# Expert rows added into the residual in place: gathered rows of x, an alternating expert order, and no buffer of expert outputs

## What is computed

```python
# hier_moe: one of 4 groups per token, then 2 of the 8 experts inside that group
g_sel = argmax(h @ w_group)
top_p, top_e = top_k(softmax(exp_logits[g_sel]), 2)      # weights = p_group * top_p / sum
eid = g_sel * 8 + top_e
# expert e on its rows, in blocks of 128:
y = (silu(h @ w_gate[e]) * (h @ w_up[e])) @ w_down[e]
x = x + sum over the token's two experts of weight * y
```

## Time and profile before

| | us |
|---|---|
| median of 3 runs | 3014.01 (3011.21 to 3019.95) |
| the profiled execution, its own time | 3014.33 |
| its span, first to last instruction | 3012.6 |
| PE busy (share of the span) | 2619.9 (87%) |
| DVE, ACT, POOL busy | 1820.9 (60%), 1647.7 (55%), 590.5 (20%) |
| the two experts stages, by their first and last POOL instructions | 1022.5 to 1570.3 and 2387.4 to 2908.9 |
| `lru`, first DVE instruction to last oT store issued | 1577.4 to 2125.9 |
| `finish`, first load issued to the end | 2915.2 to 3012.6 |

### The profile page before, as it was taken

How to read it: one execution, slowest core, us unless ns; L and a number is a source line. 1 busy time by engine, 2 the same in 40 slices (tenths; PEclk the granted TensorE clock), 3 DMA queues, 4 the chain that set the end, 5 groups by cost and what they waited for, 6 DMA issues and landing times. The chain is left out here.

```text
span 3012.6 us, 41660 instructions
## 1 busy us (share of the span) xinstructions
PE 2619.9 (87%) x12246; PEld 2100.4 (70%) x12246; DVE 1820.9 (60%) x3169; ACT 1647.7 (55%) x2260; POOL 590.5 (20%) x795
## 2 busy tenths in 40 slices
PE   6999999999799599999976999999599589999850
PEld 4878878788688477777755777777488467777640
DVE  4555555554456566565636888877465577556546
ACT  5565565554344366565635666675444376555532
POOL 0000000000011344555430000000011255545420
PEclk9999999999899799999987999999799799999985
DMA  3223223331445589789866545451444599877867
GB/s 122 90 91 101 89 91 105 104 107 57 142 155 167 173 295 312 273 281 323 271 218 215 175 166 168 144 171 63 128 154 147 178 350 337 289 264 265 307 237 293
DMA packets 388258, 573.61 MB, mean 190 GB/s; under 512 B 33408, under 2 KB 304000, under 8 KB 384000
## 3 DMA queue, kind: packets, MB, share of 16 engines
q1 hardware_dynamic: 353104, 457.23, 45.8%
q0 software_dynamic: 32688, 105.99, 9.4%
q10 hardware_dynamic: 2304, 8.39, 0.7%
HBM read 449.32 MB, written 122.22 MB: 190 GB/s over the span
## 5 line engine op out<-in xcount | busy, mean ns | idle before, releaser
L1445 DVE TENSOR_TENSOR experts_gu_lo<-carry_raw,experts_gu_hi 128x1024 fp32r<-128x1024 f32 x256 | 296.6, 1220 | 64.4 <-ACT experts_gu_hi L1404 62.4
L1327 POOL DMA_INDIRECT experts_rows<-h_rows,experts_source_now x194 | 269.8, 1391 | 274.0 <-PE experts_ps L1497 129.3
L118 PE MATMUL experts_ps<-experts_gu_hi,experts_hT_hi 128*128 128x512 f32 x760 | 316.3, 416 | 3.0 <-issue 3.0
L119 PE MATMUL experts_ps<-experts_gu_lo,experts_hT_hi 128*128 128x512 f32 x760 | 300.3, 395 | 0.0
L120 PE MATMUL experts_ps<-experts_gu_hi,experts_hT_lo 128*128 128x512 f32 x760 | 299.9, 395 | 0.0
L1404 ACT ACTIVATE experts_gu_hi<-carry_raw 128x1024 fp32r<-128x1024 f32 x256 | 250.2, 1057 | 52.5 <-DMA carry_raw<-in_moe_w_up 42.8
L1456 DVE TENSOR_TENSOR experts_hT_lo<-experts_ps,experts_hT_hi 128x512 fp32r<-128x512 f32 x194 | 133.2, 687 | 240.6 <-ACT experts_hT_hi L1383 233.6
L963 POOL MEMSET route_empty<- 128x512 int32 x2 | 1.1, 564 | 1322.1 <-POOLq L160 1322.1
L118 PE MATMUL route_ps<-route_w_hi,route_src_hi 128*128 128x512 f32 x512 | 208.6, 407 | 45.7 <-DVE route_src_lo L1029 45.7
L1396 ACT ACTIVATE experts_y<-experts_ps,experts_by_block 128x1024 f32<-128x1024 f32 x99 | 110.6, 1117 | 213.8 <-DMA y_rows<-experts_y,experts_target_now 208.4
L119 PE MATMUL route_ps<-route_w_lo,route_src_hi 128*128 128x512 f32 x512 | 203.4, 397 | 0.0
(11 more groups left out here) (322 smaller groups left out, 6757.1 us busy)
## 6 DMA issues: line engine op xcount, KB each, us to landing
carry_raw<-in_moe_w_gate SPq DMA_DIRECT2D x64, 1024.0 KB
carry_raw<-in_moe_w_up SPq DMA_DIRECT2D x64, 1024.0 KB
ahead_wd_raw<-in_moe_w_down SPq DMA_DIRECT2D x64, 1024.0 KB
gla_w_raw<-in_gla_w_in SPq DMA_DIRECT2D x32, 1024.0 KB, 7.3
ahead_wd_raw<-in_lru_w_in SPq DMA_DIRECT2D x32, 1024.0 KB
gla_w_raw<-in_gla_w_in SPq DMA_DIRECT2D x32, 512.0 KB, 5.1
route_src<-oT_rows SPq DMA_DIRECT2D x32, 512.0 KB
x_rows<-route_x_new SPq DMA_DIRECT2D x32, 512.0 KB, 2.9
```

Source lines behind the costliest of these rows:

```text
L118: nc.tensor.matmul(out, w_hi, x_hi, start=first, stop=False)
L119: nc.tensor.matmul(out, w_hi, x_lo, start=False, stop=False)
L1327: pool.indirect_dma_start(rows[:, b], None, h_halves[b], bass.IndirectOffsetOnAxis(source_now[b][:].bitcast(U32), 0))\
L1445: nc.vector.tensor_tensor(gu_lo[:, slot(e), of_part(c)], gu_raw[:, slot(e), of_part(c)], gu_hi[:, slot(e), of_part(c)].bitcast(F32), ALU.s ...
```

## The change

- Experts are taken in the order `ORDER`: expert 0 of each of the four groups, then expert 1 of each, and so on. Lists and weights are looked up by that order.
- Before a block's output is taken, POOL gathers the rows of x that it belongs to into a new buffer `acc`. DVE computes y = output x weight + acc (one instruction, L1396's work moved from ACT and joined with the addition), and POOL scatters y back over the same rows of x.
- `y_rows` is gone. `lru` and `finish` load x and go straight to the norm: no y loads, no additions, and in `lru` no store of x. The early loads of x (and in `finish` of the gain) are gone too, since x is only final when the experts are done. `finish` has 8 buffers for x, and ACT squares tile t+1 before it issues the output of tile t.
- The gathers and the scatter have a bounds check with the limit T - 1: padding places name rows from T upward and are left out of the transfer. Lists are halved in place, and the separate array of sources is gone.

```diff
+ORDER = [g * EPG + j for j in range(EPG) for g in range(GROUPS)]
 def experts
-                n = (words[e // PACK] // PACK_BASE ** (e % PACK)) % PACK_BASE
+                at = ORDER[e]
+                n = (words[at // PACK] // PACK_BASE ** (at % PACK)) % PACK_BASE
...
+            pool.memset(acc[:], 0.0)
+            pool.memset(rows[:], 0.0)
...
                 pool.indirect_dma_start(rows[:, b], None, h_halves[b],
-                                        bass.IndirectOffsetOnAxis(source_now[b][:].bitcast(U32), 0))\
+                                        bass.IndirectOffsetOnAxis(source_now[b][:].bitcast(U32), 0),
+                                        bounds_check=T - 1, oob_is_err=False)\
...
-                pool.indirect_dma_start(y_rows, bass.IndirectOffsetOnAxis(target_now[:].bitcast(U32), 0),
-                                        y[:], None).then_inc(y_stored, DMA)
+                pool.indirect_dma_start(x_rows, bass.IndirectOffsetOnAxis(target_now[:].bitcast(U32), 0),
+                                        y[:], None, bounds_check=T - 1, oob_is_err=False).then_inc(y_stored, DMA)
+            def name_acc(i):
+                if not (isinstance(i, int) and i == -1):
+                    pool.wait_ge(acc_in, nth_acc(i - 1))
+                pool.wait_ge(listed, nth(i - 2))
+                stand(pool)
+                pool.tensor_copy(acc_now[:].unsqueeze(1), by_block[:, bass.ds(i + (LAG - 2), 1), 0:1])\
+                    .then_inc(acc_set, 1)
+            def gather_acc(i):
+                pool.wait_ge(acc_set, nth(i + 1))
+                pool.wait_ge(y_done, nth(i - 1))
+                stand(pool)
+                pool.indirect_dma_start(acc[:], None, x_rows,
+                                        bass.IndirectOffsetOnAxis(acc_now[:].bitcast(U32), 0),
+                                        bounds_check=T - 1, oob_is_err=False).then_inc(acc_in, DMA)
             def each(e, b, g, n):
                 name_rows(0, column, g + 1)
                 gather(0, g + 1)
                 name_targets(g - 1)
+                name_acc(g)
                 store_y(g - 1)
+                gather_acc(g)
                 name_rows(1, column, g + 1)
                 gather(1, g + 1)
                 keep_list(column, g + 1)
...
+            def take_y(i):                      # on DVE, removed from ACT
+                dve.wait_ge(y_ps_done, nth(i))
+                dve.wait_ge(acc_in, nth_acc(i))
+                dve.wait_ge(y_stored, nth_stored(i - 1))
+                dve.wait_ge(listed, nth(i - 2))
+                stand(dve)
+                nc.vector.scalar_tensor_tensor(
+                    out=y[:].rearrange("p (b c) -> p b c", b=2), in0=ps[:, Y:Y + 2],
+                    scalar=by_block[:, bass.ds(i + (LAG - 2), 1), 1].bitcast(F32),
+                    in1=acc[:].rearrange("p (b c) -> p b c", b=2), op0=ALU.mult, op1=ALU.add).then_inc(y_done, 1)
...
             def each(e, b, g, n):               # DVE
                 take_aT(g)
+                take_y(g)
                 take_rows(g + 1, 0)
 def lru
+            def load_x(t):
+                after(sp, h_done, t - 2)
+                sp.dma_start(x[:, t % 2], x_dram[t * P:(t + 1) * P, :]).then_inc(x_in[t % 2], DMA)
-            def combine(t):
-                step(nc.vector.tensor_tensor(x[:, j], x[:, j], y_ab[:, j, 0], ALU.add))
-                nc.vector.tensor_tensor(x[:, j], x[:, j], y_ab[:, j, 1], ALU.add).then_inc(x_done, 1)
 def finish
+            for t in range(NT):
+                after(sp, h_done, t - XD)
+                sp.dma_start(x[:, t % XD], x_dram[t * P:(t + 1) * P, :]).then_inc(x_in[t % XD], DMA)
+                if t == 0:
+                    sp.dma_start(gain[:], norm_w.partition_broadcast(P)).then_inc(gain_in, DMA)
...
+                if t + 1 < NT:
+                    mean_square(t + 1)
                 after(act, h_done, t)
                 act.dma_start(out[t * P:(t + 1) * P, :], h[:, j]).then_inc(stored[j], DMA)
...
-                step(nc.vector.tensor_tensor(x[:, t % XD], x[:, t % XD], y_ab[:, j, 0], ALU.add))
-                nc.vector.tensor_tensor(x[:, t % XD], x[:, t % XD], y_ab[:, j, 1], ALU.add).then_inc(x_done, 1)
```

More of the change, by code:

```diff
@@ L1205, in project_and_route, with experts @@
         m.end()
-def experts(nc, k, stage, h_halves, lists_dram, w_gate, w_up, w_down, y_rows, ahead, after_all):
+def experts(nc, k, stage, h_halves, lists_dram, w_gate, w_up, w_down, x_rows, ahead, after_all):
     with ExitStack() as ctx:
@@ L1436, in _ @@
             take_aT(blocks)
-            for i in (blocks, blocks + 1):
-                take_y(i)
         @block.vector
@@ L1489, in _ @@
             take_aT(blocks)
+            for i in (blocks, blocks + 1):
+                take_y(i)
         @block.tensor
@@ L1769, in _ @@
             after_dma(sp, y_stored, STEPS - 1)
-            for j in range(2):
-                after_dma(sp, x_stored[j], NT // 2 - 1)
         @block.scalar
@@ L2149, in build @@
                               moe_w_down[1])
-            early = FinishEarly(nc, held)
-            experts(nc, k, "experts1", h_halves, lists, moe_w_gate[1], moe_w_up[1], moe_w_down[1], y_rows, ahead,
-                    lambda sp, _: early.load(sp, x2, final_norm))
-            finish(nc, k, x2, y_rows, early, out[0])
+            experts(nc, k, "experts1", h_halves, lists, moe_w_gate[1], moe_w_up[1], moe_w_down[1], x2, ahead,
+                    lambda sp, _: None)
+        finish(nc, k, x2, final_norm, out[0])
 INPUTS = ["x", "gla_norm", "gla_w_in", "gla_w_alpha", "gla_b_alpha", "gla_head_norm", "gla_w_out",
```

139 lines of the change are left out of this document (42 added, 97 removed).

## The result

The changed kernel takes 3070.9 us (median of 4 runs, 3067.8 to 3073.8) against 3015.8 us of the kernel before (4 runs in the same comparison): ratio 1.0183, 95% interval 1.0162 to 1.0204. It is slower by 55 us, where 11 us faster was forecast, and it lies above the range. The profiled run has a span of 3072.1 us.

A forecast was written before the change was run, and what follows sets the result against it. Experts were taken as PE-bound (91 to 93% busy) with late h rows and the output loop behind, one-block runs as weight-bound, finish as nearly DMA-bound. Terms -47 - 4 + 4 - 10 + 15 + 31 = -11 gave 3003 us, range 2950 to 3065.

The forecast's parts named there:

- 1. finish: Final stage: half the bytes per tile and two fewer DVE additions, -47 us, bounds -40 and -50.
- 2. lru: In lru: a shorter start without y loads and additions, steady steps unchanged, -4 us, bounds 0 and -29.
- 3. Ends: Ends of the experts stages: last outputs form a serial chain with the added gather, 2 us a stage, +4 us.
- 4. order: Experts of layer 1: alternating groups mixes one-block and two-block experts, relieving weight loading, -10 us, bounds 0 and -25.
- 5. y on VectorE: Experts: the output moved to DVE makes one-block experts late, half of them charged, +15 us, bounds 0 and +30.
- 6. POOL and the output loop: Experts: POOL's added copy and gather delay second blocks, 1.0 us for each of 31, +31 us, bounds 0 and +124.
- POOL becomes the bound: Experts: two-block experts pay 1.3 us a block, the others 0.9, giving 3068 us; chance 0.2.
- POOL's waits for PE vanish: Experts: sign that POOL limits the kernel, its 67.6 us of waits for PE, between scatter and second gather, disappearing.
- The experts cost nothing: Experts: left-out padding, evened DMA and POOL's room absorb the added work, giving 2957 us; chance 0.25.
- The padding still moves: Experts: out-of-bounds places cost as much as others, 1.5 us per one-block expert, giving 3053 us; chance 0.1.
- DVE waiting for the gather of x: Experts: sign that DVE's output would wait for the x gather where ACT waited for the scatter.
- PE's waits for h up from 24: Experts: sign that PE's waits for gathered rows of h would rise from 24 us.

The follow-up runs named there:

- experiment 3: The kernel before with only the order of the experts changed to alternating groups, weights and lists taken in that order: 3016.7 us (ratio 1.0008).

## Why the prediction was wrong

The forecast was -11 and the result +55 (the profiled spans differ by 59.5). By its own steps:

*1. finish, -47*: measured -49.4, within its bounds: 48.0 us from first load to end. That is 44 for the bytes, 2 before them and 2 behind, as I had them; from 2915.2 these parts end at 2963.2, and the 2965.5 that I wrote had 2 more. The rate was not as steady as I had it, 399 GB/s for 15 us and 363 for the rest, so hitting 48.0 is in part luck. The Trainium skill ("SBUF — State Buffer", "A bandwidth-pool intuition that's wrong") has about 358 GB/s between HBM and a core and would have made the term -43. The trace of the changed kernel disagrees in the first stretch and comes near it in the second.

*2. lru, -4*: measured -8.8 with the routing behind it, within the bounds. The start has the 4 us: from the first VectorE instruction to the first norm's VectorE operation it takes 6.3 us in place of 10.3. Where the rest comes from was not followed. The longer wait at the ratio, 33.6 us against 7.2, shows that the removed additions had filled a gap.

*3. Ends, +4*: from the start of PE's last product to the next stage the two layers take 15.6 and 16.4 us, 10.6 and 10.8 before. So +10.7, over twice the term. It comes with the gather of x, since with no gather they take 10.4 and 9.2.

*4. order, -10; 5. y on VectorE, +15*: together +5, and 4.7 in the kernel with no gather. That is luck. The order by itself is worth 0 to 1 us, not -10: what it gains in one stretch is not there in the rest of the stage. With that, y on VectorE, together with what left-out padding gave back, cost some 5, not 15. I had also weighed whether the new operation stretches POOL's work. With it and no gather of x, a gather of h takes 1382 ns on average, against 1391 before. The rule of the Trainium skill ("SBUF — State Buffer", "Who interferes with whom"), by which an operation with at most one SBUF input does not hold up GpSimd, agrees with that.

*6. POOL and the output loop, +31*: this is the step that failed. The gather of x measured 113 us (118 of the experts less 4.7), 11 of them at the ends, so 102 in the blocks; the bounds were 0 and 124. The price of a block was about right, and the blocks that pay it were wrong. I had the loop output, scatter, landing, output go from 9.9 to 11.1 us, and the block shown went from 10.5 to 11.7. But I charged 1.0 us for the 31 second blocks only, and nothing here for the others, since they looked as if they had room. From one split of the down weights (L1476; L1453 in the kernel of experiment 3, which has the same order and the old output) to the next, an expert with two blocks takes 23.0 us on average in place of 20.6, so 1.2 a block, and one with one block 12.1 in place of 11.3. Over 62 of the 64 experts that is 71 and 27 us.

What the 113 are made of, in the changed kernel's order: 52 us are POOL's own time, at about 0.3 of the total for each us that I had counted as room. I wrote that what lands changes little, and the total did not grow, but the bytes of the gather are worth 19 us; as an explanation, and not shown, they stand in front of a waiting reader where the padding did not. The dependence is worth 42 us, and 20 once the naming copy is moved, so these parts don't simply add up. I had also no term for the clock: of the 118 us, 31 are busy time of PE with the same instructions. No run parts it from the waits that it follows.

*The range.* Item 6 had a bound of +124, but the range stopped at 3065, just short of the dearest case by its own words, and the result lies 6 us above it.

*The rivals.* "POOL becomes the bound" gave 3068, 3 us from the result, and its prices were the better ones: 1.3 us for each block of a two-block expert and 0.9 for the others, where 1.2 and 0.9 were measured. But its sign, that POOL's waits for PE vanish, did not come: they are 118.7 us against 129.3. And its 111 us were all POOL's time, of which the runs give 52 or less; bytes and dependence made up the rest. It met the number with about half of its mechanism. "The experts cost nothing" gave 2957, which is what the kernel with no gather takes, 2957.5: what it overlooked is the gather. "The padding still moves" is out: 102.87 MB on the software queue, while x and h rows without padding are 100.7.

*The signs.* DVE waiting for the gather of x, PE's waits for h up from 24, the wait at the ratio longer: all came. A block takes longer than the 11.0 that I gave: 43 scatters in 500 us are 11.6 each, against 48 in 507, 10.6.

## What to carry to other kernels

An in-order engine that issues for two loops has no spare time just because it waits half of each block: price every added issue at a share of its time, find out that share with a plain fill at the place, and ask of the issue's landing by how much it ends later than the one that the loop already waits for. Charge it to every block until a run shows which ones have room. Before taking a read-modify-write through memory for a final pass saved, compare what the pass costs once at full bandwidth (58 us here) with what the read costs in each step's loop (113). Where every reordering only moves the wait from one loop to another, look for fewer issues. A second tile for the rows of x may help too; no run here shows it.

## What the runs showed of the hardware

- An indirect gather whose rows are all but one out of bounds costs POOL 1.16 us on average, one with its real rows 1.11 to 1.30: leaving rows out saves bytes, not issue time.
- A scatter and a gather of x issued 1.3 us apart land side by side: where POOL waited for the scatter in the changed kernel, it took note of it 7.1 to 7.7 us behind the end of the issue (7 blocks), and of the gather 5.4 to 7.8 us behind its own (12 blocks).
- A scatter that adds takes POOL 1.63 us where one that writes takes 1.03 (means of 103), and its landing keeps the next output waiting 194.0 us in place of 117.9.
- Behind a wait of 4.25 us of TensorE the granted clock stood at 0.50 for 4 us, while it was busy. In all, equal work took 31 us (3%) more of busy time in the slower kernel, and it lies in the products of down and the transposes.
- A copy of 128x1 on POOL takes 0.18 us, or 1.19 when VectorE is splitting weights beside it, as at two places of this timeline of the kernel with no gather:

```profile
1291.45 1.19 POOL L1333 COPY experts_source_now<-experts_lists 128x1 int32 x1
...
1302.05 0.18 POOL L1333 COPY experts_source_now<-experts_lists 128x1 int32 x1 [1.31 <-DMA experts_rows<-h_rows,experts_source_now]
```
